# RMS factors applied behind the products of the dense FFN and of q/k/v, with the raw residual transposed by feature halves, in a two-block fp32 kernel

## The chip, the cores and the metric

One core of a Trainium2 chip runs the whole program. The metric is the device time of one execution in microseconds (us), the median of three runs. Five engines work side by side and meet at semaphores: TensorE (PE: matrix products and transposes into the eight PSUM banks), VectorE (DVE), ScalarE (ACT), GpSimd (POOL) and SyncE (SP, which issues the weight loads). Each engine takes its instructions in the order in which they are written, so an instruction that waits for a semaphore holds up all that stand behind it on its engine.

## The reference, cut to what matters

256 tokens of 1024 features, in fp32, go through two blocks. The first has a convolution layer and an attention layer, each followed by a feed-forward part (dense, then a mixture of 8 experts); the second block is not touched by the change.

```python
def rms_norm(x, g):
    xf = x.astype(jnp.float32)
    y = xf * lax.rsqrt(jnp.mean(xf * xf, axis=-1, keepdims=True) + EPS)
    return (y * g.astype(jnp.float32)).astype(x.dtype)

def swiglu(h, w_gate, w_up, w_down):
    return (jax.nn.silu(h @ w_gate) * (h @ w_up)) @ w_down

# layer 0
x = x + conformer_conv(rms_norm(x, mix_norm[0]), ...)   # its last product is u @ w_out
x = x + swiglu(rms_norm(x, ffn_norm[0]), ...)           # 1024 -> 2816 -> 1024
# layer 1
h = rms_norm(x, mix_norm[1]);  hn = rms_norm(x, kv_norm)
q = h @ w_q;  k, v, f_logit = split(hn @ w_kvf)
logf_cum = cumsum(log_sigmoid(f_logit + b_f))
x = x + forgetting_attention(q, k, v, logf_cum) @ w_o
```

An RMS norm is `x * r * g`, with one factor `r` for each token and one gain `g` for each feature. A product over the features can therefore be made of `x * g`, and its result multiplied by `r` of its token.

## The kernel before, in words

**Products.** An fp32 product is made as three products of fp32r halves: each operand is split into a high part, made on ACT (a copy into fp32r), and a low part, made on DVE (the operand minus the high part). `three` (L2047 to L2051) issues high by high, high by low and low by high into one bank.

**Weights.** They come from memory in units of 2 MB, and each is split by halves of 2048 columns: `high_pre` (L922, line L931 in the profile) on ACT, `low_pre` (L936, line L950) on DVE. There are three buffers for split halves (SPLIT), so half h can be split only when PE has begun what follows half h - 3 (semaphore `p_used`); PE waits with `p_split` for half h. Which half is split when is written out by hand, as the places of `high_pre` and `low_pre` between the other work of ACT and DVE. Counted from 0, halves 0 and 1 are those of the second column half of w_out, 2 to 34 those of the dense FFN, 35 to 38 those of w_q, and k, v and w_o follow.

**Two kinds of product tile.** `features` (L2056) takes one half and makes 256 output features by 256 tokens in one bank: 48 products of 256 columns. `tokens` (L2072) and `down` (L2086) take one half and make products of 512 columns: 24 of them. The dense FFN (L2262 to L2269) makes its feature tiles ff0 to ff21 in pairs, and behind each pair from the second on the down product of the pair before; the 11 down products are summed in the four banks ffd, one for each half of the tokens (tt) and of the columns (c). Ahead of each down product PE waits with `f_at` until ACT and DVE have made both activation tiles of its pair.

**An activation tile.** ACT takes silu of the gate half of a bank (L978), splits the high part of the next weight half (L931), and copies the activation's high part (L982). DVE multiplies silu by the up half (L992), makes the weight's low part (L950) and the activation's low part (L996). Every second tile is followed by one more weight half on both engines.

**The norms.** Ahead of the FFN (norm 1) and ahead of q (norm 2) the order is this. `add_four` (L896, L902) adds the four banks of the product before to the residual X, 512 columns at a time. `norm_act` (L770) takes the sum of squares of each token half (L776) and its root (L781), `norm_dve` (L847) the reciprocal (L845) and the scaled rows H = X * r (L855). `norm_pe` (L873) transposes H, 16 blocks of 128x128 into four banks (L886). ACT and DVE then make the high (L793) and low parts (L834) of the transposed rows, times the gain, 256 columns at a time. Ahead of the transposes and behind them `keep_busy` (L2025, L2034) issues products whose results nobody reads.

**q, k, f and v.** q comes in four feature tiles, which ACT scales and copies by quarters (L913, L914); k in four, which DVE copies (L1411); then f and the four tiles of v (L1896), then attention.

Of the kernel before, what the change touches and what calls it, by code (L numbers as in the profile page):

```python
# [23 lines left out]
P = 128  # L24
# [8 lines left out]
DH = 64  # L33
# [136 lines left out]
def build(nc, dr, out, dbg=None):  # L170
    with ExitStack() as ctx:
# [106 lines left out]
        plan_norm(pre, 2)  # L278
        for n in range(4):
            pre.add(("q", n))  # L280
# [110 lines left out]
        SGF = big[:, 3072:4096].rearrange("p (b n) -> p b n", b=2)  # L391
        NH = mid_r[:, 0:DC * (HEADS + 2 * GH)]
# [137 lines left out]
        def _(sp):  # L530
# [81 lines left out]
            sp.wait_ge(S("h_ready"), 8)  # L612
# [62 lines left out]
        def _(pool):  # L675
# [38 lines left out]
            for tt in range(TT):  # L714
                pool.wait_ge(S("h_ready"), 7 + tt)
                pool.dma_start(dr["tokens"][tt * P:(tt + 1) * P, :], H[:, tt, :]).then_inc(S("pool_moved"), 16)
# [53 lines left out]
        def norm_act(act, B, u, ready, order, gains):  # L770

            if u in (1, 2, 3, 4):
                table_for(act, ACT.Sqrt)
# [9 lines left out]
            if u in split_base:  # L783
                for gname, pair in gains:
                    if gname == "kv":
                        high_pre(act)
                    for j in range(4):
                        bank = filled(act, B, ("T", u, j))
                        if gname != gains[0][0]:
                            act.wait_ge(S("ht_lo"), split_base[u] + 2 * j + 2)  # L790
                        for c in range(2 * j, 2 * j + 2):
                            src = bank[:, (c % 2) * SEQ:(c % 2 + 1) * SEQ].rearrange("p (t s) -> p t s", t=TT)
                            nc.scalar.activation(pair.hi[:, c], src, ACT.Copy, scale=V(gname, c)).then_inc(S("ht_hi"), 1)  # L793
            elif gains:
                if u == 0:
                    act.wait_ge(S("ld_vec"), 16)
                transposed(act, B, u, gains, 0)

# [19 lines left out]
        x_before = {1: 0, 2: 2, 3: 4, 7: 6}  # L818
        split_base = {1: 0, 2: DC, 5: 3 * DC, 7: 4 * DC}

        def lows_dve(dve, B, u, gains):

            n = split_base[u]
            for gname, pair in gains:
                final = gname == gains[-1][0]
                if gname == "kv":
                    low_pre(dve)
                for j in range(4):
                    bank = filled(dve, B, ("T", u, j))
                    n += 2  # L830
                    dve.wait_ge(S("ht_hi"), n)
                    for c in range(2 * j, 2 * j + 2):
                        src = bank[:, (c % 2) * SEQ:(c % 2 + 1) * SEQ].rearrange("p (t s) -> p t s", t=TT)
                        nc.vector.scalar_tensor_tensor(pair.lo[:, c], src, V(gname, c), pair.hi[:, c].bitcast(F32),  # L834
                                                       ALU.mult, ALU.subtract).then_inc(S("ht_lo"), 1)
                    if j and final:
                        dve.wait_ge(S("ht_lo"), n - 2)
                        dve.sem_inc(B.free[B.at[("T", u, j - 1)][0]], 1)
            dve.wait_ge(S("ht_lo"), n)
            dve.sem_inc(B.free[B.at[("T", u, 3)][0]], 1)  # L840
# [6 lines left out]
        def norm_dve(dve, ch, B, u, order, gains):  # L847
# [9 lines left out]
            if u in split_base:  # L857
                lows_dve(dve, B, u, gains)
# [32 lines left out]

        def ht_ready(pe, u, n=1):
# [3 lines left out]
        def add_four(dve, B, name, done, final):  # L896

            for tt in range(TT):
                for c in range(2):
                    bank = filled(dve, B, (name, tt, c))  # L900
                    dst = X[:, tt, c * 512:(c + 1) * 512]
                    ins = nc.vector.tensor_tensor(dst, dst, bank[:, :], ALU.add)  # L902
                    s, k = let_go(B, (name, tt, c), ins)
                    dve.wait_ge(s, k)
                dve.sem_inc(S(done), 1)

        def queries_act(act, B, name, n):

            QZ = QZS[0 if B is pre else 1]
# [62 lines left out]
        def ffn_act(act):  # L972

            table_for(act, ACT.Silu)
            for s in range(FT // 2):
                for i in (2 * s, 2 * s + 1):
                    bank = filled(act, pre, ("ff", i))
                    nc.scalar.activation(SGF[:, i % 2, 0:SEQ], bank[:, 0:SEQ], ACT.Silu).then_inc(S("f_silu"), 1)  # L978
                    high_pre(act)
                    b, k = pre.at[("ff", i)]  # L980
                    act.wait_ge(pre.free[b], k + 1)
# [4 lines left out]
        def ffn_dve(dve):  # L986

            for s in range(FT // 2):
                for i in (2 * s, 2 * s + 1):
                    bank = filled(dve, pre, ("ff", i))  # L990
                    dve.wait_ge(S("f_silu"), i + 1)
                    ins = nc.vector.tensor_tensor(PRF[:, i % 2, 0:SEQ], bank[:, SEQ:2 * SEQ], SGF[:, i % 2, 0:SEQ], ALU.mult)  # L992
                    let_go(pre, ("ff", i), ins)
                    low_pre(dve)
# [126 lines left out]
        def delta_act(act, ch):  # L1121
# [31 lines left out]
            act.wait_ge(S("ab_ready"), 1)  # L1153
# [4 lines left out]
            nc.scalar.activation(TMP[3][:, 0, :], row[:, R_ALOG:R_ALOG + GH], ACT.Exp).then_inc(S("ab_exp"), 1)  # L1158
# [16 lines left out]
            act.wait_ge(S("l2_ready"), 1)  # L1175
            nc.scalar.activation(SC2, SC2, ACT.Sqrt).then_inc(S("l2_root"), 1)
            table_for(act, ACT.Exp)

        def decays_act(act):

            act.wait_ge(S("decay_steps"), 1)
            nc.scalar.activation(SPARE[:, 0:1024], SPARE[:, 0:1024], ACT.Exp).then_inc(S("dt_ready"), 1)
# [1679 lines left out]
```

## Time and profile before

| | |
|---|---|
| median of 3 runs | 1610.15 us (1609.58 to 1611.86) |
| span of the profiled execution, first to last instruction | 1607.7 us |
| median less span (launch and end, and the difference between executions) | 2.45 us |
| PE busy | 98% of the span |
| DVE busy | 74% |
| ACT busy | 62% |
| DMA | 260 GB/s over the span |
| mean granted clock of TensorE | 0.997 of 2.4 GHz |

The profiled execution's own time is known as its span; sums over the trace are made against that, and carried over to the median as they are. A row of the timeline gives the start of an instruction (or of a run of equal ones), its duration, engine, line, operation, the tiles it writes and reads, and in brackets how long the engine stood idle before it and for whom. Successive products overlap in the records, so PE's pace is read from start to start.

### The profile page before, as it was taken

What the parts mean: (1) busy time and instruction counts of PE and PEld (TensorE: products, weight loads), DVE (VectorE), ACT (ScalarE), POOL (GpSimd) and SP (SyncE); (2) the same over time, 40 slices, a digit from 0 to 9 for tenths busy, and PEclk for the clock granted to TensorE, in tenths of its full rate; (3) what the DMA queues carried; (4) which work ended last, traced back from release to release, by engine and by line L of the source; (5) the groups of instructions that cost most, each with busy time, mean ns of one, the idle gap of its engine ahead of it and who ended that gap; (6) DMA issues with size and microseconds to landing.
All of it is one profiled execution on the core that took longest, in us unless ns stands there. A gap on an engine that the chain in (4) does not pass through costs nothing.

```text
span 1607.7 us, 25365 instructions
## 1 busy us (share of the span) xinstructions
PE 1572.2 (98%) x9910; PEld 1347.5 (84%) x9910; DVE 1182.9 (74%) x1110; ACT 991.7 (62%) x1122; POOL 94.3 (6%) x106
## 2 busy tenths in 40 slices
PE   8999999999999999999999999999999999999998
PEld 6858999898868888888888888888887998889997
DVE  5865454565568988988888888988987767755554
ACT  5455443466457777878777787777776553444443
POOL 1021000000041000101001010100211000000000
PEclk9999999999999999999999999999999999999999
DMA  9725545453159898998989899898997430245540
GB/s 342 237 80 196 196 171 184 158 210 137 61 208 404 318 418 362 387 423 333 420 332 419 359 389 424 331 422 333 391 396 273 165 118 3 81 146 195 191 176 27
DMA packets 56380, 418.61 MB, mean 260 GB/s; under 512 B 6776, under 2 KB 9680, under 8 KB 15088
## 3 DMA queue, kind: packets, MB, share of 16 engines
q1 hardware_dynamic: 52752, 406.44, 64.6%
q0 software_dynamic: 3552, 11.09, 2.2%
q8 instruction: 55, 0.90, 0.2%
q14 instruction: 21, 0.17, 0.0%
HBM read 408.48 MB, written 9.03 MB: 260 GB/s over the span
## 4 chain that ended last, share of the span: by engine, by line
PE 92%; DVE 4%; ACT 1%; issue 1%; DMA 0%; DVEq 0%; ACTq 0%; SPq 0%
PE ps L2049 27%; PE ps L2051 26%; PE ps L2050 26%; PE ps L2107 3%; PE ps L2552 2%; PE ps L2408 1%; PE ps L2123 1%; PE ps L2228 1%; PE ps L2034 0%; PE ps L2399 0%; PE ps L886 0%; ACT h_t L776 0%; DMA x_t<-in_x 0%; PE ps L2351 0%; DVE rt L1430 0%
## 5 line engine op out<-in xcount | busy, mean ns | idle before, releaser
L1079 DVE TENSOR_TENSOR wl<-raw,wh 128x2048 fp32r<-128x2048 f32 x194 | 443.9, 2292 | 65.2 <-ACT wh L1074 58.3
L2049 PE MATMUL ps<-wh,f_r 128*128 128x512 f32 x1152 | 454.2, 394 | 1.3 <-DVE wl L1079 1.3
L2050 PE MATMUL ps<-wl,f_r 128*128 128x512 f32 x1152 | 448.5, 389 | 0.0
L1074 ACT ACTIVATE wh<-raw 128x2048 fp32r<-128x2048 f32 x192 | 368.3, 1918 | 96.4 <-PE ps L2051 55.0
L2051 PE MATMUL ps<-wh,f_r 128*128 128x512 f32 x1088 | 424.3, 390 | 0.0
L2049 PEld LDWEIGHTS ps<-wh,f_r 128*128 128x128 f32 x1152 | 216.3, 188 | 46.3 <-DVE wl L1079 2.8
L2050 PEld LDWEIGHTS ps<-wl,f_r 128*128 128x128 f32 x1152 | 216.5, 188 | 43.1
L2051 PEld LDWEIGHTS ps<-wh,f_r 128*128 128x128 f32 x1088 | 204.2, 188 | 43.4
L2049 PE MATMUL ps<-ht_t_r,wh 128*128 128x256 f32 x832 | 237.4, 285 | 1.2 <-DVE h_t_r L834 1.0
L2050 PE MATMUL ps<-h_t_r,wh 128*128 128x256 f32 x832 | 236.1, 284 | 0.0
L2051 PE MATMUL ps<-ht_t_r,wl 128*128 128x256 f32 x832 | 236.0, 284 | 0.0
L950 DVE TENSOR_TENSOR wl<-raw,wh 128x2048 fp32r<-128x2048 f32 x50 | 114.5, 2292 | 85.8 <-ACT wh L931 85.6
L2049 PEld LDWEIGHTS ps<-ht_t_r,wh 128*128 128x128 f32 x832 | 160.1, 192 | 4.1 <-issue 3.2
L2050 PEld LDWEIGHTS ps<-h_t_r,wh 128*128 128x128 f32 x832 | 160.3, 193 | 1.2 <-issue 0.4
L969 DVE TENSOR_TENSOR wl<-raw,wh 128x2048 fp32r<-128x2048 f32 x48 | 109.8, 2291 | 68.7 <-ACT wh L962 68.4
L2051 PEld LDWEIGHTS ps<-ht_t_r,wl 128*128 128x128 f32 x832 | 160.2, 193 | 0.0
L931 ACT ACTIVATE wh<-raw 128x2048 fp32r<-128x2048 f32 x50 | 95.7, 1916 | 60.3 <-PE ps L2049 60.2
L1079 DVE TENSOR_TENSOR wl<-big,wh 128x2048 fp32r<-128x2048 f32 x48 | 110.1, 2293 | 16.2 <-ACT wh L1074 15.8
L962 ACT ACTIVATE wh<-raw 128x2048 fp32r<-128x2048 f32 x48 | 91.8, 1915 | 48.4 <-PE ps L2049 44.9
L1074 ACT ACTIVATE wh<-big 128x2048 fp32r<-128x2048 f32 x48 | 92.2, 1921 | 36.0 <-PE ps L2408 14.4
L2049 PE MATMUL ps<-wh,big_r 128*128 128x512 f32 x216 | 84.3, 391 | 0.0
L2050 PE MATMUL ps<-wl,big_r 128*128 128x512 f32 x216 | 84.3, 390 | 0.0
(417 smaller groups left out, 1910.7 us busy)
## 6 DMA issues: line engine op xcount, KB each, us to landing
raw<-in_ws SPq DMA_DIRECT2D x195, 1024.0 KB, 11.1
raw<-in_ws SPq DMA_DIRECT2D x49, 2048.0 KB, 7.7
big<-in_ws SPq DMA_DIRECT2D x48, 1024.0 KB, 10.9
f<-in_ws SPq DMA_DIRECT2D x24, 1024.0 KB
ring<-in_ws SPq DMA_DIRECT2D x4, 2048.0 KB, 17.4
items<-big SPq DMA_DIRECT2D x8, 512.0 KB, 13.6
gb<-in_gains SPq DMA_DIRECT2D x5, 512.0 KB, 18.5
ring<-in_ws SPq DMA_DIRECT2D x2, 1024.0 KB, 13.2
```

The costliest lines, as they stand in the source:

```text
L931: nc.scalar.activation(half_of(wh, h % SPLIT), half_of(raw, 2 * k + part), ACT.Copy).then_inc(S("p_high"), 1)
L950: nc.vector.tensor_tensor(half_of(wl, h % SPLIT), half_of(raw, 2 * ((n - N_PRE) % RAW) + part), half_of(wh, h % SPLIT).bitcast(F32), ALU.s ...
L962: nc.scalar.activation(half_of(wh, h % SPLIT), half_of(raw, 2 * (n % RAW) + part), ACT.Copy).then_inc(S("b_high"), 1)
L969: nc.vector.tensor_tensor(half_of(wl, h % SPLIT), half_of(raw, 2 * (n % RAW) + part), half_of(wh, h % SPLIT).bitcast(F32), ALU.subtract).t ...
L1074: nc.scalar.activation(half_of(wh, h % SPLIT), ring_half(h % HALVES), ACT.Copy).then_inc(S("high"), 1)
L1079: nc.vector.tensor_tensor(half_of(wl, h % SPLIT), ring_half(h % HALVES), half_of(wh, h % SPLIT).bitcast(F32), ALU.subtract).then_inc(S("sp ...
L2049: first = nc.tensor.matmul(bank, xh, h, start=start, stop=False)
L2050: nc.tensor.matmul(bank, xh, l, start=False, stop=False)
L2051: return first, nc.tensor.matmul(bank, xl, h, start=False, stop=stop)
L2107: ins = nc.tensor.matmul(bank[0:m, 0:SEQ], w(c), src[:, c, :], start=(c == 0), stop=(c == DC - 1))
L2123: ins = nc.tensor.matmul(bank[:, :], src[:, k, tt * P:(tt + 1) * P], w[:, k, :], start=(k == 0), stop=(k == DC - 1))
L2552: ins = nc.tensor.matmul(bank[half(c), h - heads[0], :], lhs[half(c), h, :], rhs[half(c), h, :], start=True, stop=True)
```

## The change

It touches norm 1 with the dense FFN, and norm 2 with q, k, f and v.

- The residual X is transposed as it is, without r. `half_pe` transposes four of its eight feature blocks (8 transposes) once the columns of that half are complete. For norm 1, the first half goes between the two halves of w_out's second column half, for norm 2 ahead of the last of the four tiles of the last down product, whose tiles are now made in the order (tt 0, c 0), (tt 1, c 0), (tt 0, c 1), (tt 1, c 1). The second half goes into `first_features`.
- `first_features` makes the first two feature tiles by quarters: the first half of the features of tile 0, the second-half transposes, the first half of tile 1, then the second halves of both. All `keep_busy` calls of the two norms, and the rows H, are gone.
- Behind these two tiles PE waits for r (`r_ready`) and spreads it over all partitions as a row over the tokens, with two products (`rows_pe`, bank R). DVE copies it into ROWS (`rows_dve`).
- DVE multiplies each FFN tile by r when it leaves PSUM: GATE and UPS, two more operations a tile. silu reads GATE, its product with UPS moves behind `low_pre`, and ACT's copy waits for that product. q, k and f are multiplied by the row on DVE (q's copies leave ACT), v by the column of factors.
- DVE adds by columns (`add_columns`), and ACT takes the sums of squares (`roots_act`) when the last columns are added.
- Some semaphores are joined (`small_ready`, `small_done`); no order changes with them.

```diff
 # plan of the banks
+        pre.add_at(("R", 1), 4)
...
+        pre.add_at(("R", 2), (pre.next + 3) % 8)
...
 # DVE
+        def add_columns(dve, B, name, c):
+            for tt in range(TT):
+                bank = filled(dve, B, (name, tt, c))
+                dst = X[:, tt, c * 512:(c + 1) * 512]
+                s, k = let_go(B, (name, tt, c), nc.vector.tensor_tensor(dst, dst, bank[:, :], ALU.add))
+                dve.wait_ge(s, k)
+                dve.sem_inc(S("x_cols"), 1)
+        def rows_dve(dve, ch, u):
+            bank = filled(dve, pre, ("R", u))
+            ch(nc.vector.tensor_copy(ROWS[u], bank[:, 0:SEQ]))
+            if u == 2:
+                ch(nc.vector.tensor_scalar(ROWS_Q, ROWS[u], DH ** -0.5, None, ALU.mult))
...
                     bank = filled(dve, pre, ("ff", i))
+                    nc.vector.tensor_tensor(GATE[:, i % 2, :], bank[:, 0:SEQ], ROWS[1], ALU.mult).then_inc(S("f_gate"), 1)
+                    ins = nc.vector.tensor_tensor(UPS[:, i % 2, :], bank[:, SEQ:2 * SEQ], ROWS[1], ALU.mult)
+                    s_up, k_up = let_go(pre, ("ff", i), ins)
+                    low_pre(dve)
                     dve.wait_ge(S("f_silu"), i + 1)
-                    ins = nc.vector.tensor_tensor(PRF[:, i % 2, 0:SEQ], bank[:, SEQ:2 * SEQ], SGF[:, i % 2, 0:SEQ], ALU.mult)
-                    let_go(pre, ("ff", i), ins)
-                    low_pre(dve)
+                    dve.wait_ge(s_up, k_up)
+                    nc.vector.tensor_tensor(PRF[:, i % 2, 0:SEQ], UPS[:, i % 2, :], SGF[:, i % 2, 0:SEQ], ALU.mult).then_inc(S("f_prod"), 1)
...
+            low_pre(dve)
+            add_columns(dve, pre, "ffd", 0)
+            lows_dve(dve, pre, 2, "mix1", HTQ, (0, 1), final=False)
+            add_columns(dve, pre, "ffd", 1)
+            lows_dve(dve, pre, 2, "mix1", HTQ, (2, 3), final=False)
+            roots_dve(dve, ch, 2)
+            rows_dve(dve, ch, 2)
+            low_pre(dve)
+            lows_dve(dve, pre, 2, "kv", HTK, range(4), True)
+            dve.wait_ge(S("pad"), 5)
+            for n in range(4):
+                queries_dve(dve, n)
                 low_pre(dve)
...
 # PE
+            tokens(pre, [("wout", tt, 1) for tt in range(TT)], HTW, 0, True, False)
+            half_pe(pe, pre, 1, 0)
+            tokens(pre, [("wout", tt, 1) for tt in range(TT)], HTW, 4, False, True)
-            keep_busy(pre, ("T", 1, 0), 3)
-            norm_pe(pe, pre, 1, 2)
-            keep_busy(pre, ("ffd", 0, 0), 1)
+            first_features(1, [("ff", 0), ("ff", 1)], HT1)
...
+                part(0, 0)
+                half_pe(pe, pre, u, 1)
+                part(1, 0)
+                part(0, 1)
+                part(1, 1)
+                rows_pe(u)
...
-            down(pre, "ffd", FT // 2 - 1, FT // 2)
+            down(pre, "ffd", FT // 2 - 1, FT // 2, lambda: half_pe(pe, pre, 2, 0))
-            keep_busy(pre, ("T", 2, 0), 2)
-            norm_pe(pe, pre, 2, 3)
-            keep_busy(pre, ("q", 0), 1)
+            first_features(2, [("q", 0), ("q", 1)], HTQ)
```

**How the order moves on DVE at the entry of the FFN.** In both pieces wl<-raw,wh is the low part of a weight half. Before, from the last addition to X to the first activation tile:

```order
L902 TENSOR_TENSOR x_t<-x_t,ps6 128x512 [waits full6,free5]
...
L845 RECIPROCAL ss<-ss 128x1 [waits root]
L855 TENSOR_SCALAR h_t<-x_t,ss 128x1024 [waits dve_steps]
...
L834 SCALAR_TENSOR_TENSOR h_t_r<-ps2,vec,ht_t_r 128x2x128
L950 TENSOR_TENSOR wl<-raw,wh 128x2048 [waits ht_lo,p_high]
L992 TENSOR_TENSOR big<-ps3,big 128x256 [waits f_silu,full3]
L950 TENSOR_TENSOR wl<-raw,wh 128x2048 [waits p_high]
L996 TENSOR_TENSOR big_r<-big,big_r 128x256 [waits f_ath]
```

With the change, from the last addition of norm 1 (ps4 is the bank R when L941 reads it):

```order
L928 TENSOR_TENSOR x_t<-x_t,ps6 128x512 [waits free4,full6]
L1000 TENSOR_TENSOR wl<-raw,wh 128x2048 [waits free6,p_high]
...
L861 RECIPROCAL ss<-ss 128x1 [waits root,dve_steps]
L941 COPY f2<-ps4 128x256 [waits dve_steps,full4]
L1000 TENSOR_TENSOR wl<-raw,wh 128x2048 [waits dve_steps,p_high]
L1040 TENSOR_TENSOR f2<-ps3,f2 128x256 [waits full3]
L1041 TENSOR_TENSOR f2<-ps3,f2 128x256
L1000 TENSOR_TENSOR wl<-raw,wh 128x2048 [waits p_high]
L1046 TENSOR_TENSOR big<-f2,big 128x256 [waits free3,f_silu]
L1048 TENSOR_TENSOR big_r<-big,big_r 128x256 [waits f_ath]
```

The second L1000 shown, weight half 4, now stands behind the copy of R, where before its counterpart stood behind the low parts of the norm.

**DVE with the change, from the last activation tile of the FFN to q.** L1046 and L1048 are the last tile's, the L1000 behind them is half 36, L928 are the additions to X, L849 the low parts of the transposed residual:

```order
L1046 TENSOR_TENSOR big<-f2,big 128x256 [waits free0,f_silu]
L1048 TENSOR_TENSOR big_r<-big,big_r 128x256 [waits f_ath]
L1000 TENSOR_TENSOR wl<-raw,wh 128x2048 [waits p_high]
L928 TENSOR_TENSOR x_t<-x_t,ps4 128x512 [waits full4]
L928 TENSOR_TENSOR x_t<-x_t,ps6 128x512 [waits free4,full6]
L849 SCALAR_TENSOR_TENSOR f1_r<-ps3,vec,ht_t_r 128x256 [waits free6,ht_hi,full3]
...
L928 TENSOR_TENSOR x_t<-x_t,ps5 128x512 [waits full5]
L928 TENSOR_TENSOR x_t<-x_t,ps7 128x512 [waits free5,full7]
...
L941 COPY big<-ps2 128x256 [waits dve_steps,full2]
L943 TENSOR_SCALAR big<-big 128x256 [waits dve_steps]
L1000 TENSOR_TENSOR wl<-raw,wh 128x2048 [waits dve_steps,p_high]
```

Before, the additions stood directly behind the last tile, and half 36 behind the low parts for q.

**PE with the change, at the end of the last down product.** L916 is a transpose of the residual, ps7 is the bank of the last down tile and then of q's tile 0:

```order
L2123 MATMUL ps5<-wh,big_r 128x512
L916 MATMUL ps3<-cst,x_t 128x128 [waits free3,x_cols]
L916 MATMUL ps3<-cst,x_t 128x128 x3
L916 MATMUL ps4<-cst,x_t 128x128 [waits free4]
L916 MATMUL ps4<-cst,x_t 128x128 x3
L2121 MATMUL ps7<-wh,big_r 128x512
...
L2121 MATMUL ps7<-ht_t_r,wh 128x256 [waits ht_lo,free7,p_split]
L2122 MATMUL ps7<-f1_r,wh 128x256
```

The transposes come before the last down tile, and q's first product waits for `free7`, which DVE gives with the addition of that tile.

## Rows read from the trace of the kernel before

**Rows 1.** The page: PE's busy share, and the engines of the chain that ended last.

```profile
PE 1572.2 (98%) x9910; PEld 1347.5 (84%) x9910; DVE 1182.9 (74%) x1110; ACT 991.7 (62%) x1122; POOL 94.3 (6%) x106
...
PE 92%; DVE 4%; ACT 1%; issue 1%; DMA 0%; DVEq 0%; ACTq 0%; SPq 0%
```

**Rows 2.** Windows over both norms: us, PE, PEld, DVE, ACT, POOL, clock, DMA share.

```profile
122.00:130.00 8.00, 6.96 (x37) 4.37 (x36) 5.62 (x13) 6.13 (x15) 0.00 (x0) 1.00 0.86 369
...
310.00:322.00 12.00, 11.31 (x56) 8.03 (x54) 6.28 (x13) 5.53 (x14) 0.00 (x0) 1.00 0.01 3
```

**Rows 3.** Timeline of PE from w_out's last product to ff0's first.

```profile
121.51 2.74 PE L2034 MATMUL ps<-cst 128*128 128x512 f32 x6
124.82 1.09 PE L886 MATMUL ps<-cst,h_t 128*128 128x128 f32 x8 [0.58 <-DVE h_t L855]
126.28 1.09 PE L886 MATMUL ps<-cst,h_t 128*128 128x128 f32 x8 [0.36 <-DVE h_t L855]
127.21 1.02 PE L2034 MATMUL ps<-cst 128*128 128x512 f32 x2
128.34 0.36 PE L2049 MATMUL ps<-ht_t_r,wh 128*128 128x256 f32 x1
```

**Rows 4.** Timeline of PE: end of the last down product, first of q.

```profile
315.32 1.88 PE L2034 MATMUL ps<-cst 128*128 128x512 f32 x4
...
320.93 0.36 PE L2049 MATMUL ps<-ht_t_r,wh 128*128 128x256 f32 x1
```

**Rows 5.** Timeline of PE: first product of a down, of the next feature tile; of k.

```profile
202.53 0.40 PE L2049 MATMUL ps<-wh,big_r 128*128 128x512 f32 x1
...
208.00 0.28 PE L2049 MATMUL ps<-ht_t_r,wh 128*128 128x256 f32 x1
...
344.19 0.28 PE L2049 MATMUL ps<-f_r,wh 128*128 128x256 f32 x1
```

**Rows 6.** Timeline of DVE: one activation tile of the FFN.

```profile
203.22 0.43 DVE L992 TENSOR_TENSOR big<-ps,big 128x256 f32<-128x256 f32 x1 [1.40 <-ACT big L978]
204.98 2.29 DVE L950 TENSOR_TENSOR wl<-raw,wh 128x2048 fp32r<-128x2048 f32 x1 [1.33 <-ACT wh L931]
207.19 0.42 DVE L996 TENSOR_TENSOR big_r<-big,big_r 128x256 fp32r<-128x256 f32 x1
```

**Rows 7.** Timeline of ACT: the same tile, and the third weight half.

```profile
202.74 0.38 ACT L978 ACTIVATE big<-ps 128x256 f32<-128x256 f32 x1 [3.27 <-PE ps L2051]
203.03 1.92 ACT L931 ACTIVATE wh<-raw 128x2048 fp32r<-128x2048 f32 x1
204.85 0.40 ACT L982 ACTIVATE big_r<-big 128x256 fp32r<-128x256 f32 x1
208.38 1.92 ACT L931 ACTIVATE wh<-raw 128x2048 fp32r<-128x2048 f32 x1 [3.13 <-PE ps L2049]
```

**Rows 8.** Timeline of DVE: an addition to X, low parts, one copy of k.

```profile
315.59 0.69 DVE L902 TENSOR_TENSOR x_t<-x_t,ps 128x512 f32<-128x512 f32 x1 [0.74 <-PE ps L2051]
...
320.30 3.23 DVE L834 SCALAR_TENSOR_TENSOR f_r<-ps,vec,ht_t_r 128x256 fp32r<-128x256 f32 x8 [1.47 <-ACT ht_t_r L793]
...
350.16 0.68 DVE L1411 COPY f<-ps 128x512 f32<-128x512 f32 x1
```

**Rows 9.** Timeline of ACT: high parts of norm 2.

```profile
319.36 3.03 ACT L793 ACTIVATE ht_t_r<-ps,vec 128x256 fp32r<-128x256 f32 x8 [1.51 <-PE ps L886]
```

**Rows 10.** Timeline of PE: the longest idle stretch of the span, and products at the router.

```profile
1416.64 1.09 PE L886 MATMUL ps<-cst,x_t 128*128 128x128 f32 x8 [1.27 <-DVE x_t L1569]
1419.82 1.29 PE L2034 MATMUL ps<-cst 128*128 128x512 f32 x2 [2.09 <-DVEq L838]
...
459.33 0.37 PE L2340 MATMUL ps<-rt,cst 128*128 128x8 f32 x2
```

**Rows 11.** Windows behind the router's products, columns as in rows 2.

```profile
462.00:464.00 2.00, 2.00 (x11) 2.00 (x11) 1.38 (x13) 0.00 (x0) 0.30 (x2) 0.50 0.00 0
464.00:466.00 2.00, 2.00 (x16) 2.00 (x15) 0.44 (x1) 0.60 (x1) 1.46 (x7) 0.77 0.00 0
```

More of the change, by code:

```diff
@@ L391, in build @@
         SGF = big[:, 3072:4096].rearrange("p (b n) -> p b n", b=2)
+        ROWS = {1: f2[:, 0:SEQ], 2: big[:, 3072:3072 + SEQ]}
+        ROWS_Q = big[:, 3072 + SEQ:3072 + 2 * SEQ]
+        GATE = f2[:, 512:1024].rearrange("p (b n) -> p b n", b=2)
+        UPS = f2[:, 1024:1536].rearrange("p (b n) -> p b n", b=2)
+        DUMP = f2[:, 1024:2048]
         NH = mid_r[:, 0:DC * (HEADS + 2 * GH)]
@@ L783, in norm_act @@
             if u in split_base:
[L784 to L793, printed above, removed]
+                highs_act(act, B, u, gains[0][0], gains[0][1])
             elif gains:
@@ L797, in norm_act, with highs_act, roots_act @@
                 transposed(act, B, u, gains, 0)
+        def highs_act(act, B, u, gname, pair, tiles=range(4), second=False):
+            for j in tiles:
+                bank = filled(act, B, ("T", u, j))
+                if second:
+                    act.wait_ge(S("ht_lo"), split_base[u] + 2 * j + 2)
+                for c in range(2 * j, 2 * j + 2):
+                    src = bank[:, (c % 2) * SEQ:(c % 2 + 1) * SEQ].rearrange("p (t s) -> p t s", t=TT)
+                    nc.scalar.activation(pair.hi[:, c], src, ACT.Copy, scale=V(gname, c)).then_inc(S("ht_hi"), 1)
+        def roots_act(act, u, order):
+            table_for(act, ACT.Sqrt)
+            for tt in range(TT):
+                act.wait_ge(S("x_cols"), cols_before[u] + 3 + tt)
+                nc.scalar.activation(DUMP, X[:, tt, :], ACT.Square, scale=D ** -0.5,
+                                     accum_out=ss[:, tt:tt + 1]).then_inc(S("sumsq"), 1)
+                act.wait_ge(S("sumsq"), 2 * order + tt + 1)
+                nc.scalar.activation(ss[:, 4 + tt:5 + tt], ss[:, tt:tt + 1], ACT.Sqrt,
+                                     bias=cst[:, EPSCOL:EPSCOL + 1]).then_inc(S("root"), 1)
         def transposed(eng, B, u, gains, half):
@@ L890, in norm_pe, with half_pe @@
                         closed(B, name, ins)
+        def half_pe(pe, B, u, half):
+            pe.wait_ge(S("x_cols"), cols_before[u] + 2 * half + 2)
+            for j in (2 * half, 2 * half + 1):
+                bank = opened(pe, B, ("T", u, j))
+                for c in range(2 * j, 2 * j + 2):
+                    for tt in range(TT):
+                        o = (c % 2) * SEQ + tt * P
+                        ins = pay(nc.tensor.transpose(bank[:, o:o + P], X[:, tt, c * P:(c + 1) * P], C("ident")))
+                closed(B, ("T", u, j), ins)
         def ht_ready(pe, u, n=1):
@@ L2084, in tokens, with down @@
                 half_used(B)
-            def down(B, name, s, steps):
+            def down(B, name, s, steps, between=None):
                 h, l = (t.rearrange("p (f n) -> p f n", f=2) for t in half_unit_of(B))
-                for tt in range(TT):
-                    for c in range(2):
+                for a in range(TT):
+                    for b in range(2):
+                        tt, c = (b, a) if between else (a, b)
+                        if between and tt and c:
+                            between()
                         bank = opened(pe, B, (name, tt, c)) if s == 0 else ps[B.at[(name, tt, c)][0]]
```

198 lines of the change are left out of this document (117 added, 81 removed).

## The prediction

> **What bounds the kernel now.** I read the page first. PE is busy for 98% of the span and holds 92% of the chain that ended last [rows 1]: what does not shorten or lengthen PE's own sequence changes nothing. The windows over the two norms come next: they are among the few places where PE falls under full business, and part of its business there is not useful work [rows 2]. The timeline of PE says what the norms cost. At norm 1, w_out's products end at 121.51 and the FFN's begin at 128.34: 6.83 us, of which two runs of 8 transposes at 1.09 us (2.18) are needed and the rest is `keep_busy` and waiting [rows 3]. At norm 2 it is 315.32 to 320.93, 5.61 us, with the same transposes [rows 4].
>
> The pace of PE follows. A down product takes 208.00 - 202.53 = 5.47 us, so one of its four tiles takes 1.37 [rows 5]. From 128.34 to 315.32 PE makes 22 feature tiles and 11 down products without a hole; (186.98 - 11 x 5.47) / 22 = 5.76 us a feature tile [rows 3 to 5].
>
> Last come the timelines of DVE and ACT in the FFN, for the handoffs. A bank is taken up 0.21 us after PE goes on to the next (202.74 against 202.53), ACT's weight half begins 0.29 after silu, DVE's 1.95 after ACT's, and the next DVE operation 2.21 after that. A third half starts 0.38 after PE's next product has begun [rows 5 to 7]. A short operation of 256 columns takes 0.42 on DVE and 0.40 on ACT. Between engines I add 0.05 (these rows give 0.03 to 0.10). Back to back on DVE I count 0.08 less than the duration.
>
> **What the change takes off PE.** The 6.83 and 5.61 us become the transposes (2.18 each) and the row of factors, R. R is two fp32 products of 128 columns; three `keep_busy` products of 512 columns took 2.74 us [rows 3], so 2 x 2.74 / 3 / 4 = 0.45. That leaves 6.83 - 2.18 - 0.45 = 4.20 and 5.61 - 2.18 - 0.45 = 2.98. The four q tiles took 344.19 - 320.93 = 23.26 us in place of 4 x 5.76 = 23.04 [rows 4, 5], the low parts being just in time; with products by feature halves these 0.2 us go as well, and I take the same for norm 1. Together PE gains 7.6 us. r itself leaves the path: its squares and roots have the 11.5 us of two product tiles to hide under.
>
> **What it adds: waits in DVE's order.** The three split buffers leave a half two product tiles of time if it starts as soon as it may. Now several halves stand behind instructions that wait for PE. In order of time:
>
> 1. *R to ff2.* Half 4, which ff2 needs, stands on DVE behind the copy of R, and R is PE's last work ahead of ff2. From R's end: 0.22 + copy 0.42 + half 2.29 + 0.06 = **2.99 us** of idle PE. Its high part on ACT is ready long before.
> 2. *down product 0.* An activation tile is now one chain over both engines: GATE 0.47, silu to high half 0.29, high to low half 1.95, low half to the product with UPS 2.21, that product 0.47, ACT's copy 0.45, DVE's low part 0.34 until the next GATE: 6.18 us a tile. Before, silu and its product ran ahead of the halves [rows 6, 7]. UPS lies beside ACT and costs nothing. Two tiles need 12.36 us after half 4; PE has 2 x 5.76 = 11.52 of work: **0.84 us**.
> 3. *Steady FFN.* A step is two tiles and a third half: 12.36 + (0.31 + 1.95 + 2.21 - 0.79) = 16.04 us against PE's 2 x 5.76 + 5.47 = 16.99. PE stays the bound, by 0.95 us a step, and the chain catches up. Nothing is lost here; were the handoffs 0.1 us longer each, ten steps would cost some 3 us.
> 4. *The last down product.* From ff20's end to tile 21's low part: 0.22 + 6.18 + 6.32 = 12.72 us, against ff21 and down product 9 with 5.76 + 5.47 = 11.23: **1.49 us**. Before, the low half was followed by one short operation and came in time.
> 5. *Transposes in the last down product.* DVE now makes half 36 ahead of the additions, and that half waits for this product's first instruction: 0.38 + 1.95 + 2.21 + two additions at 0.75 [rows 7, 8] = 6.04 us. PE wants to transpose after three tiles, 4.10: **1.94 us**.
> 6. *q's first tile.* It takes the bank of the last down tile, whose addition stands behind the low parts of the first four feature blocks. From the transposes: 0.55 + 0.22, two high parts 0.79 (3.03 us for 8), four low parts 1.60 (3.23 for 8), two additions 1.50 = 4.66 us [rows 8, 9]. PE has 1.09 + 1.37: **2.20 us**.
> 7. *R to q2.* As 1, with one more operation for ROWS_Q (0.30): **3.29 us**.
> 8. *q3.* Behind half 37 come eight low parts for k and v (3.20), the two products that write q tile 0 (1.32, by the copy of 512 columns in 0.68 [rows 8]) and half 38: 2.21 + 3.20 + 1.32 + 2.35 = 9.08 us from half 37's start, against 2.35 + 5.76: **0.97 us**. From q3 on DVE leads again.
>
> The sum of the waits is 13.7 us. Later parts only shift: f's longer way to the decays has v's products above it, v's and k's multiplications replace copies of the same size. POOL's memsets and the weight loads have tens of microseconds. The moved transposes are all counted.
>
> **Sum.** +13.7 - 7.6 = +6.1 us. The median of the runs stands 2.45 us over the profiled span; I carry the difference over unchanged: 1610.15 + 6.1 = **1616.3 us**, and a span of about 1613.8. What the trace of before does not show is bounded so: R costs between 0.27 (two transposes) and 1.8 (two whole `keep_busy` products), and I take 0.45 since its columns are those of a transpose; handoffs at 0.03 or at 0.10 move the eight waits by -0.7 or +1.7 us together; ROWS_Q costs 0.16 to 0.42. That gives 1615 to 1619.
>
> **Clock.** The longest idle stretch of PE in the trace is 2.09 us, and the granted clock stayed at 2.4 GHz there. After thin products at the router (8 columns each, with holes) it fell to 0.50, that is 1.2 GHz, for 462 to 464 and was 0.77 until 466 [rows 10, 11]. The change makes holes of 3.0 and 3.3 us, takes all `keep_busy` away, and leaves three smaller holes inside 12 us. The sum above has full clock.
> The Trainium skill ("TensorE: Matmul & The Clock Gate", section "Why this matters for your kernels") warns that idle gaps between bursts of products send the clock back to its lower level; by it the sum would be that of rival A, 1617 to 1619 us in place of 1616.3, and the trace neither bears it out nor refutes it, since no hole there is as long.
>
> **Rivals.**
>
> *A. The clock falls* after one or more of the three places. One fall costs 2 x 0.50 + 2 x 0.23 = 1.5 us of PE's work [rows 11]. After the first R, 0.84 of it is spent waiting anyway (wait 2), so 0.7; around the last down product 1.5; after the second R 0.5, since wait 8 absorbs 0.97. Time: 1617 to 1619. For it: holes longer than any before. Against: full work on both sides of each. Chance 0.26.
>
> *B. Faster: DVE has its halves ready.* The place is DVE's order around the two R and the last down product. If halves 4, 36 and 37 were split before PE wants them, waits 1, 2, 5, 7 and 8 (10.0 us) would go, and 3.7 of waits stand against a gain of 7.6: 1606.2 us. It decides from the point at which the waits sum to less than 4.4 us. For it: ACT and DVE have idle time, 26% and 38% of the span. Against: the written order puts the copy of R ahead of half 4 and 37, and no idle time can pass it. Chance 0.07.
>
> *C. Much of the waits is hidden, and the two sides nearly cancel:* waits of 4.4 to 10.8 us give 1607 to 1613.4. It needs, for one, that a bank, a semaphore or a copy is passed on much faster than in the rows. Chance 0.12.
>
> *D. It does not do what it says:* the first-half transposes wait for additions at norm 1 too, or R is late for want of roots, so that the holes stay. ACT has r some 6 us ahead of R by the rows, and DVE adds w_out's first columns while the products of the second run. It would add the 4 us of norm 1: about 1620. Chance 0.03.
>
> **How the numbers follow.** The sum as it stands has 0.52. A change of under 0.2% (3.2 us) can't be told from none here. Slower by more: the sum, A and D, 0.81. Within: C, 0.12. Faster by more: B, 0.07. The point is that of the sum, 1616.3. The range goes from 1613.0, into the upper end of C, to 1619.4, over A; under 0.2 lies outside.
>
> **What would show it.** In the profile after: PE idle for about 3.0 us ahead of ff2, for 3.3 ahead of q2, both for the low half on DVE; 0.8, 1.5, 1.9, 2.2 and 1.0 us at the other places; no `keep_busy` at the norms; w_out's end to ff0 only 0.1 us; the FFN's middle at 16.98 us a step; the stretch from w_out's last product to k's first longer by 6. The forecast is wrong if the middle of the FFN slows (wait 3), if the holes at R are under 1 us, or if the granted clock shows 0.50 in windows behind them.

## The result and the profile after

| | before | with the change |
|---|---|---|
| median of the runs, us | 1610.68 (1609.58 to 1611.86, 4 runs) | 1618.92 (1617.57 to 1619.67, 4 runs) |
| ratio to before, 95% interval | | 1.0052 (1.0038 to 1.0067) |
| span of the profiled execution, us | 1607.7 | 1616.5 |
| its mean granted clock | 0.997 | 0.994 |

The change makes the kernel slower, by 8.2 us between the medians and 8.8 between the spans. The time lies where the prediction put the waits. The page of the kernel with the change, busy time by engine and the chain that ended last, as [rows 1]:

```profile
PE 1571.2 (97%) x9904; PEld 1348.6 (83%) x9904; DVE 1202.3 (74%) x1162; ACT 987.8 (61%) x1106; POOL 103.0 (6%) x106
...
PE 91%; DVE 5%; ACT 2%; issue 2%; DMA 0%; DVEq 0%; ACTq 0%; SPq 0%
```

PE's busy time hardly falls (1571.2 against 1572.2 us), though `keep_busy` is gone at both norms: part of what it gave up came back as products that take longer at a lower clock. Its idle time grows from 35.5 to 45.3 us (span less busy time). The view of waits, PE alone (engine and line waited for: total us, times, longest), names what is new:

```profile
PE ps L2121 <- DVE wl L1000: 6.2, 2, 3.3
PE ps L916 <- DVEq L930: 2.0, 1, 2.0
...
PE ps L2121 <- DVE big_r L1048: 1.8, 2, 1.3
...
PE ps L2121 <- issue: 0.8, 1, 0.8
```

These are 10.8 us of holes, none of which was in the kernel before. The timeline of PE shows each with its place, where [rows 3] and [rows 4] showed `keep_busy` and short waits for the norms:

```profile
134.69 0.60 PE L2149 MATMUL ps<-cst,ss 128*128 128x128 f32 x4
...
138.25 0.39 PE L2121 MATMUL ps<-ht_t_r,wh 128*128 128x256 f32 x1 [2.95 <-DVE wl L1000]
...
150.57 0.50 PE L2121 MATMUL ps<-wh,big_r 128*128 128x512 f32 x1 [0.55 <-DVE big_r L1048]
...
310.41 0.50 PE L2121 MATMUL ps<-wh,big_r 128*128 128x512 f32 x1 [1.29 <-DVE big_r L1048]
...
316.80 1.45 PE L916 MATMUL ps<-cst,x_t 128*128 128x128 f32 x8 [2.01 <-DVEq L930]
...
321.64 0.36 PE L2121 MATMUL ps<-ht_t_r,wh 128*128 128x256 f32 x1 [0.83 <-issue]
...
334.11 0.60 PE L2149 MATMUL ps<-cst,ss 128*128 128x128 f32 x4
...
338.00 0.58 PE L2121 MATMUL ps<-ht_t_r,wh 128*128 128x256 f32 x1 [3.28 <-DVE wl L1000]
```

From top to bottom: R, then ff2; down product 0; the last down product; the transposes inside it; q0; the second R, then q2. The first product of q2 takes 0.58 us in place of 0.39, and the transposes of 316.80 take 1.45 in place of 1.09: the clock is low there. The windows show it, columns as in [rows 2], the clock third from the right:

```profile
134.00:140.00 6.00, 3.05 (x26) 2.85 (x25) 3.38 (x4) 1.44 (x2) 0.00 (x0) 1.00 0.00 0
...
318.00:320.00 2.00, 2.00 (x7) 1.61 (x6) 1.56 (x4) 1.98 (x4) 0.00 (x0) 0.50 1.07 459
...
338.00:340.00 2.00, 2.00 (x9) 2.00 (x10) 2.00 (x6) 0.00 (x0) 0.00 (x0) 0.50 0.00 0
```

And the timeline of DVE around the first R and the second, which shows why PE waits:

```profile
135.33 0.42 DVE L941 COPY f<-ps 128x256 f32<-128x256 f32 x1 [6.39 <-PE ps L2149]
135.90 2.29 DVE L1000 TENSOR_TENSOR wl<-raw,wh 128x2048 fp32r<-128x2048 f32 x1
138.11 0.42 DVE L1040 TENSOR_TENSOR f<-ps,f 128x256 f32<-128x256 f32 x1
...
144.27 0.42 DVE L1040 TENSOR_TENSOR f<-ps,f 128x256 f32<-128x256 f32 x1
...
334.75 0.42 DVE L941 COPY big<-ps 128x256 f32<-128x256 f32 x1 [6.63 <-PE ps L2149]
```

DVE is idle for 6.39 and 6.63 us ahead of the copies of R, with a weight half of 2.29 us queued behind each. That half (135.90 to 138.19) is what ff2 waits for. The two L1040 rows give the pace of the activation tiles: 6.16 us (prediction: 6.18).

I follow one stretch in every kernel, from the first product of w_out's second column half to k's first. It has the same products in all of them, `keep_busy`, transposes and R aside. Before it runs from 110.50 to 344.19 [rows 5], 233.69 us; with the change from 110.43 to 351.05:

```profile
110.43 0.48 PE L2121 MATMUL ps<-wh,f_r 128*128 128x512 f32 x1
...
351.05 0.28 PE L2121 MATMUL ps<-f_r,wh 128*128 128x256 f32 x1
```

That is 240.62, **+6.93 us** of the +8.8. The other 1.9 arise behind the start of attention, which the change doesn't touch (below).

### The profile page after: what moved, and what is told of

Same layout as the page of the kernel before. It is cut to its first block, busy times and chain, and to the rows that moved or that the text cites. A ratio compares the mean times of both kernels' runs of the same rounds, so it can differ in the third digit from the quotient of the medians.

```text
span 1616.5 us, 25400 instructions
## 1 busy us (share of the span) xinstructions
PE 1571.2 (97%) x9904; PEld 1348.6 (83%) x9904; DVE 1202.3 (74%) x1162; ACT 987.8 (61%) x1106; POOL 103.0 (6%) x106
## 4 chain that ended last, share of the span: by engine, by line
PE 91%; DVE 5%; ACT 2%; issue 2%; DMA 0%; DVEq 0%; ACTq 0%; SPq 0%
PE ps L2121 26%; PE ps L2123 26%; PE ps L2122 26%; PE ps L2220 3%; PE ps L2663 2%; PE ps L2519 1%; PE ps L2236 1%; PE ps L2341 1%; ACT wh L981 1%; DVE wl L1000 0%; PE ps L2510 0%; PE ps L2106 0%; DMA x_t<-in_x 0%; DVE rt L1489 0%; PE ps L2263 0%
## 5 line engine op out<-in xcount | busy, mean ns | idle before, releaser
L1000 DVE TENSOR_TENSOR wl<-raw,wh 128x2048 fp32r<-128x2048 f32 x50 | 114.5, 2292 | 77.3 <-ACT wh L981 76.5
L2121 PEld LDWEIGHTS ps<-ht_t_r,wh 128*128 128x128 f32 x832 | 161.2, 194 | 10.8 <-DVE wl L1000 6.6
L1012 ACT ACTIVATE wh<-raw 128x2048 fp32r<-128x2048 f32 x48 | 91.7, 1914 | 48.8 <-PE ps L2121 45.3
## 6 DMA issues: line engine op xcount, KB each, us to landing
f<-in_ws SPq DMA_DIRECT2D x24, 1024.0 KB, 10.8
items<-big SPq DMA_DIRECT2D x8, 512.0 KB, 13.7
```

Of the source, the lines that this page charges most:

```text
L1000: nc.vector.tensor_tensor(half_of(wl, h % SPLIT), half_of(raw, 2 * ((n - N_PRE) % RAW) + part), half_of(wh, h % SPLIT).bitcast(F32), ALU.s ...
L1012: nc.scalar.activation(half_of(wh, h % SPLIT), half_of(raw, 2 * (n % RAW) + part), ACT.Copy).then_inc(S("b_high"), 1)
L2121: first = nc.tensor.matmul(bank, xh, h, start=start, stop=False, skip_group_check=skip)
```

## The experiments

Seven kernels, each the kernel with the change and one edit or several. The edits move calls, choose other banks or, in busy_in_holes, add products that nobody reads, so the amount of useful work is the same in all.

**halves_first.** The low half stands ahead of the copy of R:

```diff
             roots_dve(dve, ch, 1)
-            rows_dve(dve, ch, 1)
             low_pre(dve)
+            rows_dve(dve, ch, 1)
...
-            rows_dve(dve, ch, 2)
             low_pre(dve)
+            rows_dve(dve, ch, 2)
```

> The change, with weight halves 4 and 37 split on DVE ahead of the copy of R instead of behind it. The stretch from w_out's first split product to k's first product was 233.7 us before and 240.6 with the change. My theory (the written order of DVE makes the waits): no idle PE ahead of ff2 and q2 (2.95 and 3.28 before that), and since the chains that follow start about 2.3 us earlier, down product 0 waits 1.3 to 1.6 us and q3 about 2.1; the stretch comes to 236.0 us, the time to 1614.3. Rival 1 (the waits are only moved): the holes at R vanish, those at down product 0 and q3 grow by as much, 240.6 and 1618.9. Rival 2 (the clock is what costs): with the long holes the low clock goes too, another 1 to 3 us, under 235 us.

Measured: 1615.14 us (1612.82 to 1616.79), ratio 1.0028 (1.0016 to 1.0041); stretch 110.08 to 348.24, 238.16 us. The 3 us holes at ff2 and q2 are gone. The timeline of PE shows R and right behind it, by 0.36 us, the product that stood 3 us away:

```profile
134.34 0.60 PE L2149 MATMUL ps<-cst,ss 128*128 128x128 f32 x4
134.70 0.36 PE L2121 MATMUL ps<-ht_t_r,wh 128*128 128x256 f32 x1
...
340.90 0.39 PE L2121 MATMUL ps<-ht_t_r,wh 128*128 128x256 f32 x1 [2.50 <-DVE wl L1000]
```

Of 6.2 us of holes the kernel got back 2.5 in the stretch. A part reappears downstream: down product 0 waits 1.39 us instead of 0.55, q3 2.50 (last row) where the change shows no wait. So rival 1, by which all of it comes back, fails, and so does rival 2. The clock is low behind q3's hole, with no wait left after it that could take the loss up:

```profile
342.00:344.00 2.00, 2.00 (x11) 2.00 (x11) 1.97 (x2) 1.30 (x1) 0.00 (x0) 0.50 0.72 205
344.00:346.00 2.00, 2.00 (x15) 2.00 (x15) 1.94 (x3) 0.00 (x0) 0.00 (x0) 0.73 1.03 442
```

These two windows lose 2 x 0.50 + 2 x 0.27 = 1.5 us, which is most of the 2.2 by which the stretch exceeds 236.0.

**half36_and_bank.** Half 36 stands behind the first two additions again, and q0 doesn't take the last down tile's bank:

```diff
-            low_pre(dve)
             add_columns(dve, pre, "ffd", 0)
+            low_pre(dve)
...
-            pre.add(("q", n))
+            pre.add_at(("q", n), (0, 1, 2, 7)[n])
+        pre.next = (pre.next + 4) % 8
```

> The change, with half 36 behind the additions of ffd's first columns instead of ahead of them, and q's tile 0 in a bank that FFN tile 21 has left (0) instead of that of the last down tile (7). Theory: the waits of 2.01 and 0.83 us around the last down tile go, and with them the 1.7 us that these instructions took longer at the low clock; q's first product comes 4.6 us earlier after the start of the last down product (11.2 us in the change, 6.6 here). The stretch to k's first product 236.0 us, time 1614.3. Rival (additions or low parts of the residual are late by themselves): the transposes or q's first products still wait 1 to 2 us, 238 us.

Measured: 1614.98 us (1613.0 to 1617.28), ratio 1.003 (1.0021 to 1.004); stretch 111.18 to 347.96, 236.78 us. The transposes inside the last down product, at 316.04, and q0 have no wait any more; the wait ahead of the last down product itself (wait 4) stays, at 1.28 us:

```profile
316.04 1.03 PE L917 MATMUL ps<-cst,x_t 128*128 128x128 f32 x8
...
318.54 0.35 PE L2122 MATMUL ps<-ht_t_r,wh 128*128 128x256 f32 x1
```

So waits 5 and 6 of the prediction come from the place of half 36 and from the bank; the two were moved together, not one by one. They were worth 3.8 us of the stretch, and more at equal clock: in this execution the clock fell behind the first R, and from ff2's first product to that of down product 0 it took 13.10 us (139.00 to 152.10) against 12.32 in the change. These 0.78 us are the whole of what the stretch has over the 236.0 expected.

**product_first.** The product of silu and UPS stands ahead of the low half, as before the change:

```diff
-                    low_pre(dve)
                     dve.wait_ge(S("f_silu"), i + 1)
                     dve.wait_ge(s_up, k_up)
                     nc.vector.tensor_tensor(PRF[:, i % 2, 0:SEQ], UPS[:, i % 2, :], SGF[:, i % 2, 0:SEQ], ALU.mult).then_inc(S("f_prod"), 1)
+                    low_pre(dve)
```

> The change, with the product of silu and UPS on DVE ahead of the weight's low part, as before the change; GATE and UPS stay. Theory: the chain of an activation tile falls from 6.18 to about 5.3 us, two tiles take 10.7, less than PE's 11.5 and 11.2: the waits of 0.55 us at down product 0 and 1.28 at the last down product go, 238.8 us for the stretch, 1617.1 us. Rival (the two more operations by themselves are what makes the chain late): both waits stay, 240.6 us.

Measured: 1617.13 us (1615.74 to 1618.71), ratio 1.0044 (1.0027 to 1.0061); stretch 110.65 to 350.22, 239.57 us, 0.8 over the expectation. Down product 0 and the last one no longer wait. The timeline of DVE, one activation tile:

```profile
138.33 0.42 DVE L1040 TENSOR_TENSOR f<-ps,f 128x256 f32<-128x256 f32 x1
...
139.23 0.43 DVE L1045 TENSOR_TENSOR big<-f,big 128x256 f32<-128x256 f32 x1 [0.16 <-ACT big L1028]
141.03 2.29 DVE L1000 TENSOR_TENSOR wl<-raw,wh 128x2048 fp32r<-128x2048 f32 x1 [1.38 <-ACT wh L981]
...
143.58 0.42 DVE L1040 TENSOR_TENSOR f<-ps,f 128x256 f32<-128x256 f32 x1
```

A tile takes 143.58 - 138.33 = 5.25 us instead of 6.16. So the order inside the tile made waits 2 and 4, and GATE and UPS by themselves did not. In this execution the clock stayed full behind the hole of 1.98 us ahead of the transposes (1.00 from 316 to 320), and q0's wait shows at its full size, 2.35 us: in the kernel with the change the slow last tile had taken up the rest of it. From 334 to 342 the clock was low, at 0.50 to 0.76, and this wasn't foreseen in the 238.8: from q2's first product to k's first it took 14.16 us (336.06 to 350.22), against 12.95 in busy_in_holes below, at full clock. Up to q2's first product the kernel is 2.16 us shorter than busy_in_holes (225.41 against 227.57), which is what waits 2 and 4 cost.

**busy_in_holes.** Nothing is reordered; `keep_busy` fills three holes:

```diff
                 rows_pe(u)
+                keep_busy(pre, ("ff", 2) if u == 1 else ("q", 2), 3 if u == 1 else 3)
...
-            down(pre, "ffd", FT // 2 - 1, FT // 2, lambda: half_pe(pe, pre, 2, 0))
+            down(pre, "ffd", FT // 2 - 1, FT // 2, lambda: (keep_busy(pre, ("T", 2, 0), 2), half_pe(pe, pre, 2, 0)))
```

> The change, with products that nobody reads in three of its holes: 3 behind each R and 2 ahead of the transposes in the last down product (0.9 us each). Theory: the low clock behind the holes at 314.8 and 334.7 us cost almost nothing, since the waits for DVE that follow took it up; the granted clock stays at 1.00 from 310 to 345 us and the stretch is 240.3 to 240.6 us. Rival A of the prediction (the clock is a cost of its own): 1.5 us a fall, 237 to 239 us. The time itself can move by another 1 to 3 us with falls elsewhere.

Measured: 1619.39 us (1616.24 to 1619.83), ratio 1.005 (1.0033 to 1.0067); stretch 110.44 to 350.96, 240.52 us, as expected. Timeline of PE, then the window over the whole stretch:

```profile
135.14 2.74 PE L2106 MATMUL ps<-cst 128*128 128x512 f32 x6
...
314.67 1.88 PE L2106 MATMUL ps<-cst 128*128 128x512 f32 x4
...
321.67 0.36 PE L2121 MATMUL ps<-ht_t_r,wh 128*128 128x256 f32 x1 [2.35 <-DVE x_t L928]
```

```profile
110.00:351.00 241.00, 234.37 (x1619) 215.42 (x1618) 143.30 (x175) 106.67 (x124) 7.18 (x4) 1.00 0.49 180
```

This is the run that separates the waits from the clock. The clock is 1.00 in the whole stretch, yet the stretch is only 0.10 us shorter than with the clock falling twice. q0 waits 2.35 us and q3 1.07 (344.03 to 345.10 in the timeline), both of which the slower products had hidden: at q0 PE's last product before the hole ends 1.5 us earlier (319.33 against 320.81), and PE stands for 1.5 us longer. From q2's first product to k's first it takes 12.95 us against 13.05 in the change: this is the 0.10.

**all_three_orders.** The three reorderings together.

> The change with the edits of halves_first, half36_and_bank and product_first together. In busy_in_holes, whose clock stayed at 1.00, the waits of PE and the reads-nobody products between them come to 13.5 us. Theory: all of them are waits of DVE's order and all go but that of q3, which is 2.5 us as in halves_first; nothing takes their place, down product 0 included. Stretch to k's first product 240.5 - 13.5 + 2.5 = 229.5 us against 233.7 before, 1606.1 us: faster than before. Rival (what the orders take out comes back as another wait, of the next engine or bank): two of the three gains of 2.5, 3.8 and 1.1 us are not additive, 233 us or more, no faster than before.

Measured: **1607.1 us** (1603.71 to 1607.66), ratio 0.9974 (0.9965 to 0.9984); stretch 109.95 to 338.70, 228.75 us (229.5 expected, 233 or more by the rival), clock 1.00 throughout. Two holes are left, 1.26 us at q3, and 0.99 us right behind R, which I hadn't expected.

**q3_too.** In addition, half 38 stands ahead of the low parts for k and v:

```diff
             rows_dve(dve, ch, 2)
+            low_pre(dve)
             lows_dve(dve, pre, 2, "kv", HTK, range(4), True)
...
                 queries_dve(dve, n)
-                low_pre(dve)
+                if n < 3:
+                    low_pre(dve)
```

> As all_three_orders, and half 38 ahead of the low parts for k and v. Theory: q3's wait of 2.5 us goes too, since the low parts for k are wanted only by k's first product 11.5 us later; PE has no hole from w_out to k, the granted clock stays at 1.00 there, the stretch is 227.0 us and the time 1603.6, 0.4% under before. That is also the test of the gain side: the prediction took 7.6 us off the two norms, the stretch would be 226.1; 227.0 would make it 6.7. Rival: k's first product now waits for its low parts or for its bank, 1 to 2.5 us, 228 to 229.5.

Measured: **1604.1 us** (1601.43 to 1604.8), ratio 0.9961 (0.9947 to 0.9974); stretch 111.26 to 338.47, 227.21 us. q3 no longer waits. The hole behind R is still there, first rows of PE, last row of DVE:

```profile
325.30 0.60 PE L2152 MATMUL ps<-cst,ss 128*128 128x128 f32 x4
326.89 0.36 PE L2124 MATMUL ps<-ht_t_r,wh 128*128 128x256 f32 x1 [0.99 <-DVEq L945]
```

```profile
320.66 2.29 DVE L1001 TENSOR_TENSOR wl<-raw,wh 128x2048 fp32r<-128x2048 f32 x1 [0.52 <-ACT wh L982]
325.94 0.42 DVE L942 COPY big<-ps 128x256 f32<-128x256 f32 x1 [2.98 <-PE ps L2152]
326.40 0.29 DVE L944 TENSOR_SCALAR big<-big 128x256 f32<-128x256 f32 x1
```

The half that q2 needs ended at 322.95. It is the copy of R and ROWS_Q that q2 waits for, which it doesn't read. They give R's bank free, number 2, and my own edit had put q2 there.

**q2_bank.** So q2 and q3 exchange their banks:

```diff
-            pre.add_at(("q", n), (0, 1, 2, 7)[n])
+            pre.add_at(("q", n), (0, 1, 7, 2)[n])
```

> As q3_too, but q2 and q3 exchange their banks (0, 1, 7, 2 in place of 0, 1, 2, 7), so that q2 no longer takes the bank of the second R. In q3_too PE stood 0.99 us before q2 (325.90 to 326.89) though the low half of q2's weights had been ready since 322.95; DVE's COPY of R and ROWS_Q's product ended at 326.69, and the bank is given free behind them. Theory (the last hole of the stretch is the bank that my own edit chose): the hole goes, and with it the 0.16 us by which back-to-back products overlap in the records: stretch 227.2 - 1.1 = 226.1 us, time 1604.1 - 1.1 = 1603.0 us. Rival (q2 waits for the order of DVE, whatever its bank): the hole stays at 0.99 and the stretch at 227.2. The difference of the times, 0.07%, is too small for the medians; the stretch decides.

Measured: **1603.16 us** (1602.55 to 1604.44), ratio 0.9953 (0.994 to 0.9967); stretch 110.94 to 336.96, 226.02 us. R and the next product on PE, and the window over the whole stretch:

```profile
325.00 0.60 PE L2152 MATMUL ps<-cst,ss 128*128 128x128 f32 x4
...
325.36 0.36 PE L2124 MATMUL ps<-ht_t_r,wh 128*128 128x256 f32 x1
```

```profile
110.00:337.00 227.00, 226.91 (x1604) 212.80 (x1603) 142.44 (x172) 104.89 (x124) 7.68 (x4) 1.00 0.52 193
```

PE is busy for 226.91 of 227.00 us, at full clock, and without `keep_busy`. So q2 waited for its bank and not for the order of DVE. The idea of the change, with its prefetches in another order, beats the kernel before by 7.6 us between the medians.

## Why the prediction was right, and where it was not

The direction and the mechanism were right, and so was the time: 1618.92 us lies in the range, 2.6 above the 1616.3. Of the 2.7 by which the span is longer than the 1613.8, 0.8 are in the stretch (+6.93 against +6.1), and the other 1.9 in a place for which the prediction has no term. By its steps:

**What the change takes off PE** (forecast 7.6 us): q2_bank has the gain and no wait. Its stretch is 233.69 - 226.02 = 7.67 us shorter than that of before. The total holds, but partly by luck. R counts 0.36 us from start to start instead of the 0.45 taken (its row says 0.60, and the next product starts before that is over). A run of eight transposes between products counts 0.79 us, not 1.09:

```profile
310.03 1.03 PE L917 MATMUL ps<-cst,x_t 128*128 128x128 f32 x8
310.82 0.48 PE L2124 MATMUL ps<-wh,big_r 128*128 128x512 f32 x1
```

By these two sizes the gain would be 6.83 + 5.61 - 4 x 0.79 - 2 x 0.36 = 8.6 us. About 0.9 us of it is lost again: the last two down products take 11.57 us without the transposes against 10.91 before, and w_out's second half and the first four feature tiles take 0.1 us more each. The 0.2 us that the prediction hoped to gain in q's tiles were not gained (23.27 against 23.26 us).

**The sum of the waits** (13.7 us): busy_in_holes has all of them and full clock. Its stretch is 240.52 - 226.02 = 14.50 us longer than that of q2_bank. So this is the term that was mis-sized, by 0.8 us. Single waits, from the rows at full clock:

| wait | forecast | hole of PE |
|---|---|---|
| 1. R to ff2 | 2.99 | 2.95 |
| 2. down product 0 | 0.84 | 0.55 |
| 3. steady FFN | 0 | 0 |
| 4. last down product | 1.49 | 1.29 |
| 5. transposes | 1.94 | 2.01 |
| 6. q0 | 2.20 | 2.35 |
| 7. R to q2 | 3.29 | 3.28 |
| 8. q3 | 0.97 | 1.07 |

The sizes are those of the profile of the change for waits 1, 2, 4, 5 and 7, and of busy_in_holes for 6 and 8. The holes add up to 13.5 us. A hole costs a little more than it measures: the records of two products back to back overlap by 0.16 us, those of R and the product behind it by 0.24 (0.60 less 0.36), and at a hole the overlap is lost too. Two times 0.24 and five times 0.16 are 1.3 us; 13.5 + 1.3 = 14.8 against the 14.5 measured. Where the forecast worked from start to start, at waits 2 and 4, its 0.84 and 1.49 stand against 0.71 and 1.45. At the other five it came short, by 0.2 to 0.3 us each with the overlap counted, 1.2 together; waits 2 and 4, sized 0.2 too high, give some of that back. Rival C, by which the waits would come to 10.8 us or less, fails by the same numbers; so does D, since the first transposes of norm 1 (115.99) and both R have no idle time ahead of them. Wait 3 was right: the down products of the middle begin at 167.66 and 184.64, 16.98 us apart, so PE stays the bound. Each cause was confirmed by an edit that removes it: waits 1 and 7 have one edit and one cause, 2 and 4 another, 8 goes with q3_too. Waits 5 and 6 have two causes, and these were only removed together.

In the profile of the change itself wait 6 shows 0.83 us and wait 8 nothing. This looks like a miss and isn't one, as busy_in_holes shows.

**The clock.** Here the prediction was wrong. It named 0.50 in windows behind the holes at R as a sign that the forecast is wrong, and behind the second R, from 338, the window has 0.50. The sign was badly chosen, since the time did not follow it. It also said that the clock stayed at 2.4 GHz behind the longest hole of before, 2.09 us. The windows up to the end of that hole have 1.00; the ones behind it, which the prediction left out, have not. The kernel before, from 1418:

```profile
1418.00:1420.00 2.00, 0.18 (x1) 0.18 (x2) 1.95 (x5) 2.00 (x7) 0.00 (x0) 1.00 0.00 0
1420.00:1422.00 2.00, 2.00 (x8) 1.40 (x9) 1.30 (x5) 2.00 (x3) 0.00 (x0) 0.66 0.00 0
1422.00:1424.00 2.00, 2.00 (x11) 2.00 (x11) 2.00 (x1) 1.74 (x1) 0.00 (x0) 0.50 0.00 0
```

The kernel before already had the fall that "the trace neither bears out nor refutes". Nor was 2.09 us the longest idle time: PE is idle for the first 6.92 us of the span, and its first transposes then take 1.94 us in place of 1.09, though the window there says 1.00:

```profile
6.92 1.94 PE L886 MATMUL ps<-cst,h_t 128*128 128x128 f32 x8 [6.92 <-DVE h_t L855]
```

With the row from 1420 rival A should have had more than its 0.26, and its mechanism did come: the clock fell at two of its three places. That is also what the section "Why this matters for your kernels" of "TensorE: Matmul & The Clock Gate" in the Trainium skill warns of, idle gaps between bursts; behind the second R the trace agrees (3.28 us, then 0.50), behind the first R (2.95 us, then 1.00) it does not. But A's price was wrong too. It counted 1.5 us around the last down product; the runs show 0.10 us for the whole stretch, since PE was early for q0 by more than it lost, and for q3 by all but that 0.10. The forecast time of A, 1617 to 1619, holds the result, but not for A's reason.

**The rest of the difference.** The stretch gives +6.93, the span +8.8. Attention begins at 391.85 before and at 398.70 after, +6.85, so the excess arises behind it. A part is a clock that fell elsewhere, in stretches with the same products and the same holes. At the end of attention there is a hole of 1.00 us ahead of transposes, and then come the first products of w_o; before, then after:

```profile
425.84 0.63 PE L2199 MATMUL ps<-cst,ht_t 128*128 128x128 f32 x4 [1.00 <-DVEq L1451]
...
428.15 0.39 PE L2051 MATMUL ps<-wh,h_t_r 128*128 128x512 f32 x1
```

```profile
432.68 0.63 PE L2312 MATMUL ps<-cst,ht_t 128*128 128x128 f32 x4 [1.00 <-DVEq L1510]
...
435.02 0.63 PE L2123 MATMUL ps<-wh,h_t_r 128*128 128x512 f32 x1
```

0.39 and 0.63 us for the same product. In exchange the fall of before at the router [rows 11] is missing after. Behind the hole of 2.10 us that ends at 1427.43 (the 2.09 of [rows 10]), the clock is low for longer than before (0.68, 0.50, 0.50, 0.61 in four windows from 1426 against 0.66, 0.50, 0.98 in three from 1420), and there the distance grows from 7.6 us to 8.8 at the end. Whether such falls belong to the change stays open, since there is one profile of each kernel. But the other profiles bear on it: outside the stretch (span less stretch) before takes 1374.0 us, the change 1375.9, and the seven kernels of the experiments, which have the same code there as the change, 1374.4 to 1376.8. So this part moves by 2.4 us with nothing changed in it, and the 1.9 us are no larger than that. The interval of the ratio, 6.1 to 10.8 us, contains both 6.9 and 8.8.

**Rival B** decided "from the point at which the waits sum to less than 4.4 us" and priced the kernel with the halves in time at 1606.2. As a forecast of the change it was rightly given little. Its mechanism is what all_three_orders shows: with the halves in time the kernel is faster than before. That 1607.1 us lies so near 1606.2 is chance, since that kernel isn't B's: it is also rid of waits 4 and 6, which B keeps (3.7 us), and has two holes of 1.26 and 0.99 us instead. B also gave the idle shares the wrong way round: by [rows 1] ACT is idle for 38% and DVE for 26%.

## What to carry to other kernels

When a value is moved to the place where its consumers leave PSUM, look at what stands behind the copy of that value in its engine's order: a prefetch that doesn't need it should go first, since in-order engines turn one late operand into a late everything. A bank has the same power as a queue; a tile that takes the bank of an operation still waiting for PE waits with it, even if it reads nothing of it. And before pricing a fall of the clock, find the next wait behind it: what is lost ahead of a wait that ends on another engine costs nothing until that wait is used up, so filling the hole with dummy products buys nothing there either. Where that wait is too short, or none follows, the fall is paid: 0.8 us in half36_and_bank, 1.2 in product_first, 1.5 in halves_first.

## What was unexpected of the hardware

- The granted clock did not follow the length of the hole alone. Behind the first R, a hole of 2.95 us left it at 1.00 in the kernel with the change (row 134 to 140 above), while in half36_and_bank, with the same hole (2.96) and the same work around it, it fell:

```profile
140.00:142.00 2.00, 2.00 (x12) 2.00 (x12) 0.44 (x1) 1.53 (x1) 0.00 (x0) 0.55 0.00 0
142.00:144.00 2.00, 2.00 (x13) 2.00 (x12) 2.00 (x2) 0.00 (x0) 0.00 (x0) 0.59 0.00 0
```

- A hole of 2.01 us ahead of eight transposes brought 0.50 in one kernel, one of 1.98 at the same place left 1.00 in another (product_first). Holes of 1.00 us could bring a fall and could leave none.
- A fall that is seen in 2 us windows loses 1.7 us of PE's work (before 1420 to 1426: 0.68 + 1.00 + 0.04). In the change's stretch two falls together changed the time by 0.10 us; single ones cost 0.8 to 1.5 us where the waits behind them were missing or shorter than the loss.
